# A transformer block on one core: 144 tokens by gathered rows instead of 128, and eight gathered rows under way instead of four

## What is computed

```python
vals, idx = lax.top_k(sc, 16)                  # per token, head and half, of 128 keys
best, pos = lax.top_k(cand, 16)                # of the 16 x 16 sums
eidx = jnp.take_along_axis(cidx, pos, axis=-1) # expert = i * 128 + j
g = jax.nn.softmax(best, axis=-1)
...
ue = jnp.take(u, it, axis=0)                   # [tokens, 8*16, 1024]
act = jax.nn.gelu(jnp.einsum("td,tkd->tk", xt, ue), approximate=False) * gt
ve = jnp.take(v, it, axis=0)
return jnp.einsum("tk,tkd->td", act, ve)
```

## Time and profile before

| | |
|---|---|
| median of 3 runs | 1687.42 us |
| the profiled execution: its time / its span | 1689.35 us / 1687.5 us |
| TensorE busy (matmul) | 1635.2 us, 97% |
| VectorE busy | 1376.5 us, 82% |
| ScalarE busy | 584.1 us, 35% |
| GpSimd busy | 415.5 us, 25% |
| moved by DMA | 388.51 MB |

### The profile page before, as it was taken

The page is one execution under the profiler, slowest core; times in us unless marked ns, Lnnn a source line. Parts: engine busy times, 40 slices in busy tenths (PEclk is TensorE's granted clock), DMA queues, the critical chain, the costliest instruction groups (busy, mean ns, idle before and its releaser), DMA issues. The chain is left out here.

```text
span 1687.5 us, 23884 instructions
## 1 busy us (share of the span) xinstructions
PE 1635.2 (97%) x7985; PEld 1360.0 (81%) x7985; DVE 1376.5 (82%) x2828; ACT 584.1 (35%) x824; POOL 415.5 (25%) x375
## 2 busy tenths in 40 slices
PE   6999999989999999999999999999999999999997
PEld 4877764755445999988989889898889898898986
DVE  6787857757998999977888787878888887888876
ACT  3335653232112666652222222322222222223223
POOL 0000000012553000003333333333335444444310
PEclk7999999989999999999999999999999999999999
DMA  9522125532221455579898979787898988899971
GB/s 376 187 102 75 57 112 168 189 125 66 91 69 50 150 194 206 188 268 317 326 322 289 324 271 319 277 315 290 288 321 313 327 299 315 309 337 349 330 250 50
DMA packets 138151, 388.51 MB, mean 230 GB/s; under 512 B 9440, under 2 KB 58720, under 8 KB 132064
## 3 DMA queue, kind: packets, MB, share of 16 engines
q1 hardware_dynamic: 100064, 251.27, 41.7%
q0 software_dynamic: 36864, 134.23, 21.9%
q10 hardware_dynamic: 1152, 2.10, 0.3%
HBM read 358.20 MB, written 29.36 MB: 230 GB/s over the span
## 5 line engine op out<-in xcount | busy, mean ns | idle before, releaser
L862 PE MATMUL ps<-Vs,As 128*128 128x512 f32 x2304 | 544.6, 392 | 3.6 <-DVE Vs L1650 3.6
L812 PE MATMUL ps<-xs,Us 128*128 128x384 f32 x2880 | 523.6, 336 | 0.3
L812 PEld LDWEIGHTS ps<-xs,Us 128*128 128x128 f32 x2880 | 503.2, 188 | 9.1 <-DVE Us L1605 1.1
L862 PEld LDWEIGHTS ps<-Vs,As 128*128 128x128 f32 x2304 | 432.9, 189 | 91.3 <-issue 4.3
L1162 ACT ACTIVATE att<-ps 128x384 f32<-128x384 f32 x96 | 47.3, 492 | 590.0 <-PE ps L812 590.0
L536 POOL DMA_INDIRECT big<-pv,islot x128 | 164.1, 1282 | 215.0 <-DVE low L1669 178.2
L536 POOL DMA_INDIRECT big<-pu,islot x128 | 144.3, 1127 | 221.1 <-DVE dot L1655 186.3
L1641 DVE TENSOR_TENSOR att<-att 128x384 f32<-128x384 f32 x96 | 53.4, 556 | 137.7 <-ACT att L1162 132.6
L590 PE MATMUL ps<-big 128*128 128x512 f32 (+1 forms) x384 | 157.0, 568 | 7.7 <-ACT big L904 5.6
L1669 DVE SCALAR_TENSOR_TENSOR low<-big,act_w,low 128x1024 f32<-128x1024 f32 x128 | 158.3, 1279 | 6.0 <-DMA big<-pv,islot 5.6
L1650 DVE TENSOR_TENSOR Vs<-big,Vs 128x1024 fp32r<-128x1024 f32 x128 | 156.0, 1219 | 0.0
(11 more groups left out here) (195 smaller groups left out, 1773.7 us busy)
## 6 DMA issues: line engine op xcount, KB each, us to landing
big<-puT SPq DMA_DIRECT2D x128, 512.0 KB, 4.7
big<-pv SPq DMA_DIRECT2D x64, 1024.0 KB, 9.1
big<-stream SPq DMA_DIRECT2D x31, 1024.0 KB, 5.3
gmat<-big SPq DMA_DIRECT2D x12, 2048.0 KB, 7.3
att<-gmat SPq DMA_DIRECT2D x31, 768.0 KB, 9.5
low<-wada SPq DMA_DIRECT2D x28, 512.0 KB, 4.7
work<-wada SPq DMA_DIRECT2D x12, 512.0 KB, 5.1
big<-wada SPq DMA_DIRECT2D x8, 512.0 KB, 13.5
```

The lines of the kernel that those rows point to most:

```text
L812: mm = nc.tensor.matmul(ps[:, 6 + e, 0:DT], a, xs[:, b, k, :], start=(k == 0 and a is hi and b == 0), stop=(k == KT - 1 and a is lo))
L862: mm = nc.tensor.matmul(ps[:, 2 * b + half, :], a, Vs[:, e, w, half * T:(half + 1) * T], start=(opens and a is hi and w == 0), stop=(last ...
```

## The change

`XTOK` = 16 more tokens, 128 to 143, go by gathered rows. For them the partition is (head, token): 8 heads x 16 tokens fill the 128 partitions, and 16 slots hold the 16 experts of each head. They come first, so there are NROWS = 144 slots in each of the two passes. Their token vectors must stand once per head: ScalarE spreads them (`nrep`), TensorE transposes them (8 matmuls with the identity), ScalarE copies them to `n_ext`. Their indices and weights come by 16 small DMAs. The sum over the heads is made by two matmuls with a 0/1 matrix `gath` in the last turn, straight into the PSUM banks of the dense output. The dense side keeps its shapes for `output`, but `hidden` and `hidden_gap` compute only the columns 16 to 383, and the first four groups of G are not built (`BUILT` = 92); the 16 columns of PSUM are zeroed once. `ROWBUF` is 8: four more buffers each, in `low` for u rows and in `big` for v rows. VectorE's turns are written out; 144 dots lie in the blocks 2 to 59 and 144 adds in the blocks 60 to 121, 2 or 3 per block; the Gelu of the dots (which is now taken on `dots`, and written without the copies of `dots_out`) moves from block 64 to block 60.

```diff
-ROWBUF = 4
+ROWBUF = 8
 DOTS = 8
-ADDS = 36
+XTOK = 16
+NROWS = XTOK + SLOTS
+UB = 60
+VE = 122
...
+SKIP = XTOK // 4
+BUILT = GROUPS - SKIP
...
+        u_row = [row[:, q, :] for q in range(4)] + [low[:, q * D:(q + 1) * D] for q in range(4)]
+        v_row = [row[:, q, :] for q in range(4)] + [big[:, (10 + q) * D:(11 + q) * D] for q in range(4)]
...
         def rest_after(n):
-            return (n - GAP) * GROUPS // (EARLY + 1 - GAP) + 1
+            return (n - GAP) * BUILT // (EARLY + 1 - GAP) + 1
...
# SyncE
+            sp.wait_ge(list_in, 1)
+            for h in range(PH):
+                sp.dma_start(act_w[h * XTOK:(h + 1) * XTOK, 0:TOPK], gw[0:XTOK, 1, h, :]).then_inc(ext_here, 16)
+            sp.wait_ge(idx_ready, 2)
+            for h in range(PH):
+                sp.dma_start(eidx[h * XTOK:(h + 1) * XTOK, 0:TOPK], eidx1[0:XTOK, h * TOPK:(h + 1) * TOPK]
+                             ).then_inc(ext_here, 16)
...
# GpSimd
-            with pool.Fori(0, SLOTS // (2 * DOTS)) as it:
-                fetch(pv, it, SLOTS)
+            pool.wait_ge(alo_ready, EVERY * (-(-4 * D // DT)) + 3)
+            with pool.Fori(0, NROWS // (2 * DOTS)) as it:
+                fetch(pv, v_row, it, NROWS)
...
# TensorE
-                        mm = nc.tensor.matmul(ps[:, 6 + e, 0:DT], a, xs[:, b, k, :],
+                        mm = nc.tensor.matmul(ps[:, 6 + e, XTOK:DT], a, xs[:, b, k, XTOK:DT],
...
+            for e in range(2):
+                nc.tensor.matmul(ps[:, 6 + e, 0:XTOK], zeros[:, :], ones[:, 0:XTOK], start=True, stop=True)
             for n in range(GAP - 1):
+                if n == 2:
+                    pe.wait_ge(sc_ready, PH + 1)
+                    pe.wait_ge(spread_ready, 1)
+                    for k in range(KT):
+                        mm = nc.tensor.matmul(ps[:, 4 + k // 4, k % 4 * P:(k % 4 + 1) * P], nrep[:, k, :], ident[:, :],
+                                              start=True, stop=True)
+                    mm.then_inc(spread_done, 1)
                 hidden_gap(n)
...
+                    if last and d == 2:
+                        pe.wait_ge(row_used, NROWS + XTOK)
+                        for half in range(2):
+                            nc.tensor.matmul(ps[:, half, :], gath, acc_ext[:, half * T:(half + 1) * T],
+                                             start=False, stop=False)
...
# ScalarE
+                    if weigh and d == UB % BODY:
+                        act.wait_ge(row_used, NROWS)
+                        f(dots[:, :], dots[:, :], ACT.Gelu).then_inc(gelu_ready, 1)
...
# VectorE
+            for g in range(TURNS):
                 for d in range(BODY):
...
+                    if 2 <= o < UB:
+                        for r in range(NROWS * (o - 2) // (UB - 2), NROWS * (o - 1) // (UB - 2)):
+                            dot(r)
+                    if o == UB:
+                        row_weights()
+                    if UB <= o < VE:
+                        for r in range(NROWS * (o - UB) // (VE - UB), NROWS * (o - UB + 1) // (VE - UB)):
+                            add_row(r)
```

More of the change, by code:

```diff
@@ L536, in fetch @@
                         nc.gpsimd.indirect_dma_start(
-                            out=row[:, r % ROWBUF, :], out_offset=None, in_=table,
+                            out=places[r % ROWBUF], out_offset=None, in_=table,
                             in_offset=bass.IndirectOffsetOnAxis(ap=islot[:, half, s:s + 1], axis=0)
@@ L841, in _ @@
             nc.tensor.sem_inc(oh_used, 12)
-            for i in range(GROUPS):
+            for i in range(BUILT):
                 c = i % 4
@@ L1606, in rest_early @@
                                 ).then_inc(ulo_early, 1)
-            for i in range(GROUPS):
-                c = i % 4
-                dve.wait_ge(oh_used, i + 1 + 8)
+            for j in range(BUILT):
+                c, i = j % 4, j + SKIP
+                dve.wait_ge(oh_used, j + 1 + 8)
                 v.tensor_tensor(ohj[:, 4 * c:4 * c + 4, :], iotan[:, :].unsqueeze(1).broadcast_to([P, 4, NK]),
@@ L1651, in weigh @@
                                 ).then_inc(vlo_ready, 1)
-            def dot(g, s):
-                dve.wait_ge(row_here[s % ROWBUF], g * (16 * DOTS // ROWBUF) + (s // ROWBUF + 1) * 16)
-                v.tensor_tensor_reduce(out=row[:, s % ROWBUF, :], in0=row[:, s % ROWBUF, :], in1=n_tok, scale=1.0, scalar=0.0,
-                                       op0=ALU.mult, op1=ALU.add, accum_out=dot1[:, s:s + 1]).then_inc(row_used, 1)
-            def dots_out(g):
-                dve.wait_ge(row_used, g * DOTS + DOTS)
-                v.tensor_copy(dots[:, bass.ds(g * DOTS, DOTS)], dot1[:, :]).then_inc(dots_ready, 1)
-                dve.wait_ge(dots_ready, g + 1)
@@ L1663, in add_row, with row_wait @@
[L1663 to L1671 removed]
+            def row_wait(r):
+                dve.wait_ge(row_here[r % ROWBUF], 16 * (r // ROWBUF + 1))
@@ new lines, in dot, with row_weights @@
+            def dot(r):
+                if r == 0:
+                    dve.wait_ge(ext_ready, 1)
+                row_wait(r)
+                v.tensor_tensor_reduce(out=u_row[r % ROWBUF], in0=u_row[r % ROWBUF],
+                                       in1=n_ext if r < XTOK else n_tok, scale=1.0, scalar=0.0,
+                                       op0=ALU.mult, op1=ALU.add, accum_out=dots[:, r:r + 1]).then_inc(row_used, 1)
+            def row_weights():
+                step(v.memset(acc[:, 0, :], 0.0))
+                step(v.memset(acc[:, 1, :], 0.0))
+                step(v.memset(gath, 0.0))
+                settled()
+                step(v.tensor_reduce(gath[:, 0:XTOK], ident[:, :].rearrange("p (h t) -> p t h", h=PH), axis=AX.X, op=ALU.add))
+                dve.wait_ge(gelu_ready, 1)
+                dve.wait_ge(ext_here, 16 * 2 * PH)
+                step(v.tensor_tensor(act_w[:, :], act_w[:, :], dots[:, :], ALU.mult))
+                settled()
@@ L1688, in norm @@
                                        ).then_inc(y_out, 1)
-            def dense_turn(g, rows, last=False, first=False):
+            for g in range(TURNS):
                 for d in range(BODY):
-                    nxt = d + 1
-                    if nxt % EVERY != EVERY - 1 and not (last and nxt == BODY):
+                    o, nxt = g * BODY + d, d + 1
+                    if nxt % EVERY != EVERY - 1 and o + 1 < XT:
                         i = nxt - nxt // EVERY
@@ L1696, in dense_turn @@
                     weigh(g, d)
-                    if first:
-                        for s in range(4 * DOTS * max(d - 2, 0) // (BODY - 2), 4 * DOTS * max(d - 1, 0) // (BODY - 2)):
-                            dot(s // DOTS, s % DOTS)
-                            if s % DOTS == DOTS - 1:
-                                dots_out(s // DOTS)
-                    elif rows is dot:
-                        for s in (2 * (d % 4), 2 * (d % 4) + 1):
-                            dot(g * 4 + d // 4, s)
-                        if d % 4 == 3:
-                            dots_out(g * 4 + d // 4)
-                    elif not last:
-                        for s in range(ADDS * d // BODY, ADDS * (d + 1) // BODY):
-                            add_row(g, s)
-                    else:
-                        left = SLOTS - ADDS * (TURNS // 2 - 1)
-                        for s in range(2 * d, min(2 * d + 2, left)):
-                            add_row(g, s)
-                        if d == BODY - 5:
-                            dve.wait_ge(row_used, 2 * SLOTS)
-                            step(v.tensor_tensor(acc[:, 0, :], acc[:, 0, :], acc[:, 1, :], ALU.add))
-                            dve.wait_ge(h_here, 16)
-                        if d == BODY - 4:
-                            residual(0)
-                        if d == BODY - 2:
-                            norm(0)
@@ new lines, in _ @@
+                    if o == UB:
[3 more added lines that the diff above has]
+                            add_row(r)
+                    if o == XT - 5:
+                        dve.wait_ge(row_used, 2 * NROWS)
+                        step(v.tensor_tensor(acc[:, 0, :], acc[:, 0, :], acc[:, 1, :], ALU.add))
+                        dve.wait_ge(h_here, 16)
+                    if o == XT - 4:
+                        residual(0)
```

107 lines of the change are left out of this document (60 added, 47 removed).

## The result

The changed kernel takes **1674.61 us** (median of 6 runs, 1673.33 to 1676.55), beside 1687.35 us for the kernel before (6 runs, 1686.38 to 1690.63): a ratio of 0.992, 95% interval 0.991 to 0.9931. It is 12.7 us faster. The forecast was 19.4 us, 1668; the range and the direction hold.

What follows compares the result with a forecast made beforehand. TensorE was taken to bound the kernel from 509 us on. The terms -19.4 - 1.8 - 3.7 + 3.8 + 1.5 sum to -19.6 us, giving 1668 us, with an 8-in-10 range of 1663 to 1681.

Steps and rivals of the forecast that it cites:

- Part 1: Hidden blocks on TensorE: 16 columns fewer save 0.164 us a block, 118 blocks give -19.4 us.
- A: Rival, hidden blocks: the weight load is the floor, 368 columns keep 174.2 ns, no gain, 1687 us; chance 0.07.
- Parts 1 and 3: One-hot stage: 24 narrower hidden blocks and four groups of G fewer (-3.7 us) make it about 7.6 us shorter.
- The gap ahead of the first output: TensorE's wait for the load of G before the first output: longer by 0.3 us, not shorter.
- part 2: Early hidden blocks on TensorE: 8 narrower blocks with 128 records save 1.8 us.
- part 4: Added TensorE work: identity matmuls 2.02 us, zeroing 0.1, sum over heads 1.7; +3.8 us in all.
- Part 5: VectorE's added rows: a third row on 13 blocks with o mod 4 = 2 makes rest_u late, +1.5 us.
- Rival B: In the 13 three-row blocks TensorE waits the whole row: 15 us instead of 1.5, 1681 us; chance 0.12.
- Part 6: More transfers, 339 GB/s in the first half and 327 in the second: taken to cost 0.
- C: Rival, first half of the dense stage: transfers bound it, 32.6 us more at 314 GB/s, 1700 us; chance 0.06.
- Part 7: Eight rows under way: spare VectorE 2.1 us of waits, worth 0; starting burst could show 0 to 6 us, taken 0.
- rival D: The burst of eight rows delays the first dense blocks by up to 6 us, about 1673 us; chance 0.05.

Runs made afterwards that it cites:

- experiment 11: Changed kernel with row depth raised four to eight over 32 rows, no three-row block at o mod 4 = 2, round_u ahead of gelu_early: 1663.76 us.
- experiment 6: Changed kernel with ScalarE rounding the next u block (round_u) ahead of gelu_early among the one-hot groups: 1670.64 us.
- experiment 12: Kernel before the change with one edit, round_u ahead of gelu_early on ScalarE while the groups are built: 1685.30 us against 1688.39.
- experiment 7: Changed kernel with three instead of four one-hot scalings in 84 groups, so a quarter of G is wrong: 1674.65 us.
- experiment 1: Changed kernel with four row buffers instead of eight, all else as changed: 1698.54 us.
- experiment 5: Changed kernel with the first sixteen rows let go gradually and no third row on blocks with o mod 4 = 2: 1671.07 us.
- experiment 3: Changed kernel with the rows placed so that a block with o mod 4 = 2 never has three: 1672.29 us.

## Why the prediction was right, and where it was not

The sign, the mechanism and the order of size were right: TensorE bounds, its columns cost time, and the added rows and transfers lie beside it. Of the 19.6 us, 14.2 came in the profiled executions (12.7 by the medians; the profiled execution of the kernel before lies 2 us above its median).

- **Part 1, the columns.** Right, a little small. In experiment 11, where nothing is late, the 94 hidden blocks of the dense stage take 376.50 us in sum, before 393.62: 0.182 a block instead of 0.164. The matmuls went from 174.4 ns to 166.9, so 0.47 ns a column, not the 0.427 taken from the earlier trace rows; a flat price for the weight load (A) is excluded, and so is, for these matmuls, the slope of 0.13 of the page "TensorE: Matmul & The Clock Gate" of the Trainium skill, section "Back-to-back issue gap".
- **Parts 1 and 3 among the groups.** The terms were right (7.75 us in experiments 6 and 12), the path was not. The step that failed is "VectorE's own work shrinks there as well, so it stays just behind TensorE": it weighed two engines by their busy time, and did not follow the loop hidden, Gelu, `round_u`, `rest_early`, hidden, which runs through ScalarE, an engine busy for two thirds of that time. It bound three cycles before, and seven now, each by 0.34 to 0.38 us: the stage gave 4.7 us instead of 7.6, 2.9 lost. VectorE's load has a smaller part in what is left (experiment 7).
- **The gap ahead of the first output.** Predicted a longer wait, measured 1.25 us less, with a first output 1.13 us shorter. I draw nothing from it: the wait was 1.8 to 4.2 us in the profiles of this study, and what ends it is a load of G. Likewise part 2 and the first of part 4: the stage begins 0.8 us earlier, where 0.3 later was predicted, and executions differ there by more (551.0 to 555.5 us in the profiles). These 3.5 us are luck as far as the prediction goes: without them the time would be about 1678, 10 us beside the forecast and still in the range.
- **Part 4, the sum over heads.** 1.31 us and 0.40 in the next output: the 1.7 predicted.
- **Part 5, the third row.** Right place, 13 blocks, too small. Against experiment 11 the late hidden blocks cost 1.2 us and the outputs about them 2.0: 3.2 instead of 1.5. Rival B, a row's full length each, did not come.
- **Part 6, transfers.** Right: 335 to 342 GB/s are carried with TensorE at full time, and experiment 11 carries 350. C is refuted as a matter of rate.
- **Part 7, eight rows.** Here the prediction failed twice, in opposite senses. "They can spare VectorE 2.1 us of waits": that was the wait at 2 rows a block; at 2.48 with four buffers it is 50 us on VectorE and 29 us of the time (experiment 1). This error did no harm, since the change had the buffers. "I take 0, since the v blocks then loaded are needed two blocks later" did: rival D, given 0.05, is what happened, at 5.2 of its 6 us, though not in every execution (0.9 to 7.6 us in five profiles). The slack was counted for v alone; but v waits in SyncE's queue behind a load of G that itself took twice its time.

Together: -19.6, + 2.9 (loop), + 5.2 (D), + 1.7 (part 5), less 1.7 (columns), less 2.4 (the gap and the first output), less 1.1 (start of the stage), + 0.6 (the other outputs, 4.13 us instead of 4.12) is -14.4, against -14.2 measured.

## What to carry to other kernels

Before a shorter instruction on the bounding engine is booked as gain, follow the loop from its result back to its next input through every engine on the way, however idle that engine is on average: among the groups ScalarE was busy for two thirds of the time, and the loop through it set the pace of every third cycle. Deeper buffers have two prices, the steady one (how many must be under way at the new rate, worth 29 us here) and that of their filling, which takes bandwidth from the next loads and did best here let out over 32 rows. And in these runs it was the load in short runs of 512 bytes that suffered from the burst on the other queue, with what stood behind it. Last, one profile of each kernel is thin ground for a loss that differs between executions, as the stall does.

## What the runs showed of the hardware

- What a queue gets beside a burst on another depends on its runs. With eight gathered rows in runs of 4 KB under way and G in runs of 512 bytes, SyncE's queue moved 1.60 MB in the 16.9 us from the issue of G (1.83 to 2.03 in four other profiles); with G in long runs 2.86. The Trainium skill, page "DMA: Bandwidth & Descriptors", section "Queues, rings and completion order", says that each DMA engine goes round robin between the queues that have work for it, a whole packet at a time; the rows agree in direction, but how large a turn is no run here shows.
- 392 GB/s over 30 us into one core (experiment 5), and 350 over 240 us beside a full TensorE. The 358 GB/s of the same page, section "Where 436 GB/s comes from", weighed in the prediction, is exceeded in the first; the load of G then landed after 21.9 us and the v load behind it after 24.3, where both take about 10 (the medians of the changed kernel).
- A short idle time can cost twice. After the 3.40 us at block 4 TensorE's clock was lower for the next matmuls: PEclk 0.72 over the 6 us from 779 (between the two levels of 1.2 and 2.4 GHz, so each for a part of it), 1.00 again from 785 us on. That made 1.67 of the 5.2 us, and 2.95 of the 7.6 in experiment 3, where the idle time was 4.46. The length of the idle time alone does not decide it: after the 2.25 us ahead of the first output of the changed kernel the clock fell (second row), after 2.78 us at the same place in experiment 11 it did not (third row, from that run).

```profile
779.00:785.00 6.00, 5.97 (x20) 4.79 (x21) 5.82 (x11) 1.54 (x3) 3.56 (x3) 0.72 0.54 163
745.40:748.80 3.40, 3.40 (x9) 2.66 (x10) 0.00 (x0) 0.38 (x1) 0.41 (x2) 0.57 0.87 357
742.60:745.60 3.00, 3.00 (x14) 2.47 (x15) 0.00 (x0) 0.00 (x0) 0.19 (x1) 1.00 0.94 386
```
